# Down phases of a decoder layer: later loads of residual quarters and matrix pieces, and additions spread over steps

## The chip, the cores and the metric

The kernel runs on one core of a Trainium2 chip, in one launch. The metric is device time in microseconds; the median of three runs of the kernel before is 1755.11 us (1754.42 to 1756.94). Five engines with queues of their own share the work: TensorE (PE; its weight load is PEld), VectorE (DVE), ScalarE (ACT), GpSimd (POOL), and SyncE (SP), which issues nearly all DMAs.

## The reference

One layer over x of 1024 tokens by 1024 features, fp32:

```
x = x + 0.5 * swiglu(rmsnorm(x), w_gate1, w_up1, w_down1)      # f = 0
h = rmsnorm(x); P = h @ w_in                                   # the mixer:
x = x + concat(sliding-window attention, gated linear attention, memory attention) @ w_out
x = x + 0.5 * swiglu(rmsnorm(x), w_gate2, w_up2, w_down2)      # f = 1
swiglu(x, g, u, d) = (silu(x @ g) * (x @ u)) @ d,   inner width 2816
```

The change is in the last product of each swiglu, `... @ w_down`, with its `x + 0.5 *`: here called the down phase. There are two, f = 0 (449.6 to 669.2 us of the span) and f = 1 (1532.6 to 1748.8 us).

## The kernel before

**Precision.** Every product is made of three matmuls: each operand is split into a high part (fp32r) and the rest, and high x high, high x low and low x high are summed in PSUM (lines 56 to 58). ACT writes the high part (line 857, `down_op_hi`), DVE subtracts it from the source to get the low part (line 861, `down_op_lo`).

**A down phase** multiplies w_down (2816 x 1024) by the activations (2816 x 1024 tokens) as a 2 x 2 block product with seven products in place of eight (Strassen's scheme in Winograd's form), in the order P1, P2, P6, P5, P7, P4, P3. Each product is 11 steps; step q, from 0 to 76, takes one 128 x 512 tile of w_down (or of a sum of its quarters) as weights in four pieces of 128 columns, and one moving tile of 128 x 512 activations: 4 x 3 = 12 matmuls, each group of three called a tile here. P1, P6, P7 and P4 accumulate in PSUM banks 4 to 7 (`DOWN_X`), P2, P5 and P3 in banks 0 to 3 (`DOWN_Y`). P1, P2 and P5 start their banks anew; the others go on with what is there.

**Operands.** Step q uses operand k = 2q (weights) and k = 2q + 1 (moving tile), in a ring of ten slots, so operands are made five steps ahead. The moving tiles lie in DRAM (`act_dram`) and come back one by one: `load_b(k)` on SP waits until the step that used the slot is done (`down_free`), then issues 256 KB. w_down lies in SBUF in quarters "11", "12", "21", "22" of 11 tiles, loaded in pieces c = 0, 1, 2 of 4, 4 and 3 tiles (`load_wd`, 1 MB or 0.75 MB). In between DVE forms sums of quarters: S3 at steps 5 to 15 (line 868), S2 and S4 at 17 to 27 (lines 878, 881), S1 at 26 to 36 (line 885).

**Additions.** When a product that completes an output quarter (or a part of it) is through, DVE adds 0.5 times its four banks to four tiles of the residual in `xT` (line 908, `down_add`). The residual is loaded again in quarters of 1 MB (`load_x`, halves of features mh and of tokens h). The product that next uses the banks waits for the additions: P6, P5, P7, P4 and P3 wait for those of P1, P2, P6, P7 and of P5 in this order (line 922 and after, `down_added`). Between P7 (steps 44 to 54) and P4 (steps 55 to 65) there is no other product, and both use banks 4 to 7.

**Order of work.** All is written out by hand: `down_vector` is DVE's order, `down_scalar` ACT's, `down_sync` SP's, `down_tensor` PE's. DVE at iteration q makes operands 2q + 10 and 2q + 11; these need step q to be done. In phase f = 0, ACT also squares and scales finished residual tiles for the mixer (`SQUARE_AT`, `SPLIT_AT`), POOL sums them, and POOL makes `spans_raw` from `masks_f` once that has landed.

Of the kernel before, what the change touches and what calls it, by code (L numbers as in the profile page):

```python
# [23 lines left out]
PAIRS = F // (2 * P)  # L24
# [18 lines left out]
RING, DOWN_RING, LEAD = 7, 10, 5  # L43
# [4 lines left out]
DOWN_STEPS = PAIRS * len(DOWN_PRODUCTS)  # L48
# [12 lines left out]
def build(nc, x_in, mem_in, w_gate1, w_up1, w_down1, w_proj, w_mem, w_out, w_gate2, w_up2, w_down2, gains_in,  # L61
# [3 lines left out]
    with ctx:  # L65
# [26 lines left out]
        def place(at, *tensors):  # L92

            skip = [(f"skip{next(places)}", [P, at // 4], F32)] if at else []
            return phase(*skip, *tensors)[len(skip):]
# [44 lines left out]
        masks_f, spans_raw = place(120 * KB, ("masks_f", [P, LEVELS, P], F32), ("spans_raw", [P, LEVELS, P], F32))  # L140
# [26 lines left out]
        DOWN_X, DOWN_Y = 4, 0  # L167
# [43 lines left out]
        masks_landed, span_built, spans_stored = sem("masks_landed"), sem("span_built"), sem("spans_stored")  # L211
# [16 lines left out]
        def upper(t, l):  # L228

            s = P >> (l + 1)  # L230
            return t.rearrange("p (a u c) -> p a u c", u=2, c=s)[:, :, 1, :]
# [578 lines left out]
        def down_slot(k):  # L810
            return (k + RING) % DOWN_RING
# [28 lines left out]
        def down_source(f, k):  # L840

            (name, _), j, moving = down_item(k)
            if moving or name == "P6":
                return down_raw[:, down_slot(k), 1, :]
            return wd_tile(f, {"P1": "11", "P2": "12", "P5": "21", "P7": "11", "P4": "22", "P3": "12"}[name], j)
# [13 lines left out]
        def down_op_lo(dve, f, k):  # L859
            dve.wait_ge(op_hi, Base(f).down_op + k + 1)  # L860
            nc.vector.tensor_tensor(down_ring[:, down_slot(k), 1, :], down_source(f, k),  # L861
                                    down_ring[:, down_slot(k), 0, :].bitcast(F32), ALU.subtract).then_inc(op_ready, 1)
# [20 lines left out]
        def down_s1(dve, f, j):  # L883
            dve.wait_ge(wd_summed["S3"], Base(f).wd_sum + j + 1)
            nc.vector.tensor_tensor(wd_tile(f, "21", j), wd_tile(f, "21", j), wd_tile(f, "22", j), ALU.add
                                    ).then_inc(wd_summed["S1"], 1)


        EVICTS = {"P1": (0, 0, 0, DOWN_X), "P2": (4, 0, 0, DOWN_Y), "P6": (8, 0, 1, DOWN_X), "P7": (12, 1, 1, DOWN_X),
                  "P4": (20, 1, 0, DOWN_X), "P3": (24, 0, 1, DOWN_Y)}  # L890
        FINAL = {(0, 0): 4, (1, 1): 16, (1, 0): 20, (0, 1): 24}

        def x_final(f, m, h):
            return Base(f).evict + FINAL[m // 4, h] + m % 4 + 1

        def down_add(dve, f, p, n, mh, h, bank, j):
            b = Base(f)
            m = 4 * mh + j
            if j < 3:
                dve.wait_ge(tile_done, b.tile + 3 * p + j + 1)  # L900
            else:
                dve.wait_ge(step_done, b.step + PAIRS * (p + 1))
            if j == 0:
                dve.wait_ge(xr_landed[2 * mh + h], 16 * (f + 1))
            if n in (4, 16, 20, 24):
                dve.wait_ge(down_added, b.evict + {4: 0, 16: 12, 20: 0, 24: 8}[n] + j + (1 if n != 20 else 0))
            dst = part(xT, m, h)
            nc.vector.scalar_tensor_tensor(out=dst, in0=ps[:, bank + j, :], scalar=0.5, in1=dst,
                                           op0=ALU.mult, op1=ALU.add).then_inc(down_added, 1)
# [38 lines left out]
        def down_vector(dve, f):  # L948
            b = Base(f)
            for k in range(NEARLY, DOWN_RING):  # L950
                down_op_lo(dve, f, k)
            for q in range(DOWN_STEPS):
                if f == 0 and q == 40:
                    dve.wait_ge(masks_landed, 16)
                    for l in range(SPLITS):
                        nc.vector.tensor_copy(masks[:, l, :].rearrange("p (a c) -> p a c", c=P >> (l + 1)),
                                              upper(masks_f[:, l, :], l)).then_inc(masks_ready, 1)
                name = DOWN_PRODUCTS[q // PAIRS][0]
                if q % PAIRS == PAIRS - 1 and name != "P5":
                    n, mh, h, bank = EVICTS[name]  # L960
                    for j in range(4):
                        down_add(dve, f, q // PAIRS, n, mh, h, bank, j)
                    if name == "P7":
                        for j in range(4):
                            down_add(dve, f, q // PAIRS - 1, 16, 1, 1, DOWN_Y, j)
                if 0 <= q - 17 < PAIRS:
                    down_s24(dve, f, q - 17)
                for k in (2 * q + DOWN_RING, 2 * q + DOWN_RING + 1):
                    if k < 2 * DOWN_STEPS:
                        down_op_lo(dve, f, k)  # L970
                if 0 <= q - 5 < PAIRS:
                    down_s3(dve, f, q - 5)
                if 0 <= q - 26 < PAIRS:
                    down_s1(dve, f, q - 26)
                if f == 0:
                    for c in LOW_AT.get(q, ()):
                        norm_vector(dve, 1, *norm_steps(1)[c])

        def load_wd(sp, f, q, c):

            rows = ffn_weights[f][2].rearrange("(j p) m -> p j m", p=P)
            j0 = PAIRS if q[1] == "2" else 0
            half = slice(0, HALF) if q[0] == "1" else slice(HALF, D)
            for j in range(4 * c, min(4 * c + 4, PAIRS)):
                sp.dma_start(wd_tile(f, q, j), rows[:, j0 + j, half]).then_inc(wd_landed[q][c], 16)  # L985

        def load_b(sp, f, k):
            (_, r), j, _ = down_item(k)
            down_free(sp, f, k)
            sp.wait_ge(act_stored[r], 16 * (Base(f).pair + j + 1))  # L990
            sp.dma_start(down_raw[:, down_slot(k), 1, :], act_rows(r, j)
                         ).then_inc(b_landed[down_slot(k) // 2], 16)

        def load_x(sp, f, mh, h):
            src = (x_in, x_dram)[f].rearrange("(m p) t -> p m t", p=P)
            sp.dma_start(xT[:, 4 * mh:4 * mh + 4, h * HALF:(h + 1) * HALF],
                         src[:, 4 * mh:4 * mh + 4, h * HALF:(h + 1) * HALF]).then_inc(xr_landed[2 * mh + h], 16)

        def down_sync(sp, f):
            b = Base(f)  # L1000
            sp.wait_ge(prod_done, b.prod + OPS * (PAIRS - 1) + 4)
            for c in range(3):
                load_wd(sp, f, "11", c)
            load_b(sp, f, 1)
            sp.wait_ge(prod_done, b.prod + OPS * (PAIRS - 1) + 6)
            load_wd(sp, f, "21", 0)
            for k in (3, 5, 7):
                load_b(sp, f, k)
            load_wd(sp, f, "12", 0)
            for r in ("B22", "B21"):  # L1010
                store_act(sp, f, r, PAIRS - 1)
            load_b(sp, f, 9)
            load_wd(sp, f, "12", 1)
            for r in ("T1", "T2", "T3", "T4"):
                store_act(sp, f, r, PAIRS - 1)
            load_b(sp, f, 11)
            load_wd(sp, f, "12", 2)
            load_b(sp, f, 13)
            load_wd(sp, f, "21", 1)
            load_b(sp, f, 15)  # L1020
            for r in ("B11", "B22", "B21", "T1", "T2", "T3", "T4"):
                sp.wait_ge(act_stored[r], 16 * (b.pair + PAIRS))
            load_x(sp, f, 0, 0)
            load_b(sp, f, 17)
            load_wd(sp, f, "21", 2)
            for c in range(3):
                load_b(sp, f, 19 + 2 * c)
                load_wd(sp, f, "22", c)
            for c, (mh, h) in enumerate(((0, 1), (1, 1), (1, 0))):
                load_b(sp, f, 25 + 2 * c)  # L1030
                load_x(sp, f, mh, h)
            load_b(sp, f, 31)
            if f == 0:
                sp.dma_start(masks_f[:], masks_in).then_inc(masks_landed, 16)
            for k in range(33, 2 * DOWN_STEPS, 2):
                load_b(sp, f, k)
                if f == 0 and k in (91, 97, 103):
                    sp.wait_ge(masks_ready, SPLITS)
                    sp.wait_ge(bias_stored, 16)
                    unit_sync(sp, (k - 91) // 6)  # L1040
# [64 lines left out]
        def part(tensor, m, h):  # L1105
            return tensor[:, m, h * HALF:(h + 1) * HALF]
# [1286 lines left out]
```

## Time and profile before

| what | value |
| --- | --- |
| median of 3 runs | 1755.11 us |
| the profiled execution | 1753.94 us, its span 1752.1 us |
| PE / PEld / DVE / ACT / POOL busy | 97% / 79% / 65% / 41% / 30% |
| mean granted clock of PE | 0.993 |
| DMA over the span | 191.69 MB, 109 GB/s |
| moving tiles from act_dram | 154 issues of 256 KB |

Times of the trace are from the start of the span; 1.84 us of the profiled execution lie outside it. A matmul's duration in the trace (0.39 us) overlaps its neighbours; what counts is the distance of starts. A PE start that is late behind its neighbour is a loss, and the bracket behind a row names the releaser. "DMA share" is the busy share of the core's 16 DMA engines.

### The profile page before, as it was taken

Reading aid. Unit: us, or ns where it says so; the run is one execution under the profiler, and the core shown is the slowest. Engines: PE = TensorE matmul, PEld = TensorE weight load, DVE = VectorE, ACT = ScalarE, POOL = GpSimd, SP = SyncE. Lnnn points to the kernel's source line nnn. Section 1 sums busy time; section 2 is a strip of 40 time slices with the busy share of each in tenths; the row PEclk is TensorE's granted clock in tenths of the full one; section 3 lists DMA queues with packets and bytes.
Section 4 is the critical chain, followed back from the end, with each engine's and each line's share of the span. In section 5 each row is a group of like instructions: output and inputs, shape, how many; then the busy total and the mean of one; then the engine's idle time right before and its main releaser. Section 6 shows DMA issues by size and latency. Waiting matters only on the chain.

```text
span 1752.1 us, 24811 instructions
## 1 busy us (share of the span) xinstructions
PE 1708.0 (97%) x8295; PEld 1385.7 (79%) x8295; DVE 1131.4 (65%) x1582; ACT 718.6 (41%) x1350; POOL 532.4 (30%) x432
## 2 busy tenths in 40 slices
PE   7999999999999999999989999999999999999999
PEld 4888888888778789887756678888888888878877
DVE  8975556545499686247868872986565555559654
ACT  5533333333344463142257842443333333334442
POOL 0454455444130141000036612045554444310000
PEclk9999999999999999999989999999999999999999
DMA  7142222334853331120100032223223322593334
GB/s 200 59 162 91 102 90 98 116 122 144 312 196 99 121 98 66 49 84 24 37 1 2 14 121 90 79 84 104 90 102 118 116 102 90 173 378 95 98 91 162
DMA packets 101693, 191.69 MB, mean 109 GB/s; under 512 B 11491, under 2 KB 13972, under 8 KB 101612
## 3 DMA queue, kind: packets, MB, share of 16 engines
q1 hardware_dynamic: 100528, 188.48, 31.4%
q0 software_dynamic: 848, 2.10, 0.9%
q8 instruction: 47, 0.77, 0.2%
q14 instruction: 34, 0.28, 0.0%
q10 hardware_dynamic: 236, 0.06, 0.0%
HBM read 139.74 MB, written 50.86 MB: 109 GB/s over the span
## 4 chain that ended last, share of the span: by engine, by line
PE 91%; DMA 3%; DVE 2%; ACT 2%; POOL 1%; issue 1%; SPq 1%; ACTq 0%; DVEq 0%
PE ps L56 28%; PE ps L58 28%; PE ps L57 28%; DMA down_raw<-act_dram 3%; PE ps L1595 1%; PE ps L1566 1%; PE ps L1286 1%; ACT glu L1730 1%; POOL Pg L1933 1%; PE ps L1547 1%; PE ps L2298 1%; PE ps L1644 0%; PE ps L1632 0%; PE ps L1365 0%; SPq L985 0%
## 5 line engine op out<-in xcount | busy, mean ns | idle before, releaser
L488 DVE TENSOR_TENSOR ring<-w_raw,ring 128x512 fp32r<-128x512 f32 x240 | 238.0, 1006 | 219.4 <-ACT ring L483 219.2
L58 PE MATMUL ps<-hiT,ring 128*128 128x512 f32 x672 | 261.4, 389 | 0.0
L56 PE MATMUL ps<-hiT,ring 128*128 128x512 f32 x672 | 261.4, 389 | 0.0
L56 PE MATMUL ps<-down_ring 128*128 128x512 f32 x616 | 242.5, 394 | 10.0 <-DVE down_ring L861 5.8
L57 PE MATMUL ps<-loT,ring 128*128 128x512 f32 x640 | 249.0, 389 | 0.0
L57 PE MATMUL ps<-down_ring 128*128 128x512 f32 x616 | 240.5, 390 | 0.0
L58 PE MATMUL ps<-down_ring 128*128 128x512 f32 x616 | 240.3, 390 | 0.0
L56 PE MATMUL ps<-hiB,ring 128*128 128x512 f32 x576 | 224.9, 390 | 0.0
L58 PE MATMUL ps<-hiB,ring 128*128 128x512 f32 x576 | 224.1, 389 | 0.0
L483 ACT ACTIVATE ring<-w_raw 128x512 fp32r<-128x512 f32 x240 | 150.5, 628 | 175.8 <-PE ps L58 163.4
L861 DVE TENSOR_TENSOR down_ring<-down_raw,down_ring 128x512 fp32r<-128x512 f32 x176 | 126.9, 732 | 124.9 <-ACT down_ring L857 124.7
L857 ACT ACTIVATE down_ring<-down_raw 128x512 fp32r<-128x512 f32 x176 | 108.6, 629 | 233.2 <-DMA down_raw<-act_dram 183.7
L504 POOL TENSOR_TENSOR w_raw<-w_raw 128x512 f32<-128x512 f32 x40 | 58.3, 1461 | 313.4 <-DVE ring L488 295.2
L57 PE MATMUL ps<-loB,ring 128*128 128x512 f32 x384 | 149.4, 389 | 0.0
L56 PEld LDWEIGHTS ps<-down_ring 128*128 128x128 f32 x616 | 115.9, 188 | 41.2 <-DVE down_ring L861 17.5
L56 PEld LDWEIGHTS ps<-hiT,ring 128*128 128x128 f32 x672 | 126.1, 188 | 26.3 <-issue 0.2
L58 PEld LDWEIGHTS ps<-hiT,ring 128*128 128x128 f32 x672 | 126.1, 188 | 26.1
L57 PEld LDWEIGHTS ps<-loT,ring 128*128 128x128 f32 x640 | 120.1, 188 | 25.1
L58 PEld LDWEIGHTS ps<-down_ring 128*128 128x128 f32 x616 | 116.0, 188 | 24.3
L57 PEld LDWEIGHTS ps<-down_ring 128*128 128x128 f32 x616 | 116.1, 188 | 23.7
L56 PE MATMUL ps<-hT_hi,p_hi 128*128 128x512 f32 x320 | 132.3, 413 | 2.5 <-DVE p_lo L1216 2.5
L56 PEld LDWEIGHTS ps<-hiB,ring 128*128 128x128 f32 x576 | 108.1, 188 | 22.8 <-issue 0.5
(257 smaller groups left out, 3015.9 us busy)
## 6 DMA issues: line engine op xcount, KB each, us to landing
down_raw<-act_dram SPq DMA_DIRECT2D x154, 256.0 KB, 2.6
w_raw<-in_w_gate SPq DMA_DIRECT2D x88, 256.0 KB, 3.0
w_raw<-in_w_up SPq DMA_DIRECT2D x88, 256.0 KB, 3.2
act_dram<-actT SPq DMA_DIRECT2D x88, 256.0 KB, 2.0
act_dram<-act SPq DMA_DIRECT2D x66, 256.0 KB, 2.0
wd<-in_w_down SPq DMA_DIRECT2D x44, 256.0 KB, 5.5
wd_mirrored<-in_w_down SPq DMA_DIRECT2D x33, 256.0 KB, 5.8
p_raw<-in_w_proj SPq DMA_DIRECT2D x15, 512.0 KB, 3.6
```

Source lines behind the costliest of these rows:

```text
L56: nc.tensor.matmul(out, w_hi, x_hi, start=first, stop=False, skip_group_check=resumed)
L57: nc.tensor.matmul(out, w_hi, x_lo, start=False, stop=False, skip_group_check=resumed)
L58: return nc.tensor.matmul(out, w_lo, x_hi, start=False, stop=last, skip_group_check=resumed)
L483: nc.scalar.activation(ring[:, e % RING, 0, :], op_source(e), ACT.Copy).then_inc(op_hi, 1)
L488: nc.vector.tensor_tensor(ring[:, e % RING, 1, :], op_source(e), ring[:, e % RING, 0, :].bitcast(F32), ALU.subtract).then_inc(op_ready, 1)
L504: nc.gpsimd.tensor_tensor(w_of(x, "11"), w_of(x, "11"), w_of(x, "21"), ALU.subtract).then_inc(w_summed, 1)
L857: nc.scalar.activation(down_ring[:, down_slot(k), 0, :], down_source(f, k), ACT.Copy).then_inc(op_hi, 1)
L861: nc.vector.tensor_tensor(down_ring[:, down_slot(k), 1, :], down_source(f, k), down_ring[:, down_slot(k), 0, :].bitcast(F32), ALU.subtract ...
L1286: nc.tensor.matmul(head_bank(i, w), head_ones[:, :], head_buffer(i, w), start=True, stop=True).then_inc(head_summed, 1)
L1547: mm = nc.tensor.matmul(ps[:, SCORE_BANK[u] + g, at], qT[r, 2 * u + jj, blk(n)], kT[r, keys], start=True, stop=True)
L1566: mm = nc.tensor.matmul(ps[:, SPAN_BANK + c, :], log_a[:, n, :], spans[:, 4 * c:4 * c + 4, :], start=True, stop=True)
L1595: tr = nc.tensor.transpose(ps[:, TURN_BANK[u] + kt, i * P:(i + 1) * P], P_of[u][:, i, kt * P:(kt + 1) * P], ident[:, :])
```

## The change

Two edits, for both phases.

SP's order: before, all pieces of w_down and all four residual quarters were issued behind the first moving tiles, up to k = 29. Now they are issued behind fixed moving tiles: the pieces by `WD_BEHIND` (k = 17 to 43), the residual quarters by `X_BEHIND` (k = 21, 55, 79, 113). As load_b(k) waits for step (k - 11) / 2 to be done, each piece now has a place in time too. The masks (f = 0) come behind k = 35 instead of 31.

DVE's order: before, the four additions of a product stood together, ahead of the operands of the product's last iteration, and those of P5 behind those of P7. Now those of P1, P2, P6 and P5 stand one by one behind the operands of four iterations, those of P7 between the two operands of iteration 53, those of P4 and P3 as before.

```
-                if q % PAIRS == PAIRS - 1 and name != "P5":
+                if name in ("P4", "P3") and q % PAIRS == PAIRS - 1:
                     n, mh, h, bank = EVICTS[name]
                     for j in range(4):
                         down_add(dve, f, q // PAIRS, n, mh, h, bank, j)
-                    if name == "P7":
-                        for j in range(4):
-                            down_add(dve, f, q // PAIRS - 1, 16, 1, 1, DOWN_Y, j)
...
                     if k < 2 * DOWN_STEPS:
                         down_op_lo(dve, f, k)
+                    if k == 2 * (AT_ONCE * PAIRS + PAIRS - 2) + DOWN_RING:
+                        n, mh, h, bank = EVICTS["P7"]
+                        for j in range(4):
+                            down_add(dve, f, AT_ONCE, n, mh, h, bank, j)
+                p, j = (q + 1) // PAIRS - 1, (q + 1) % PAIRS
+                if p in LATER and j < 4:
+                    n, mh, h, bank = LATER[p]
+                    down_add(dve, f, p - (p == AT_ONCE), n, mh, h, bank, j)
...
+        WD_BEHIND = {17: ("21", 2), 19: ("12", 1), 25: ("12", 2), 29: ("22", 0), 37: ("22", 1), 43: ("22", 2)}
+        X_BEHIND = {21: (0, 0), 55: (0, 1), 79: (1, 1), 113: (1, 0)}
...
-            load_wd(sp, f, "12", 1)
...
-            load_wd(sp, f, "12", 2)
...
-            load_x(sp, f, 0, 0)
-            load_b(sp, f, 17)
-            load_wd(sp, f, "21", 2)
-            for c in range(3):
-                load_b(sp, f, 19 + 2 * c)
-                load_wd(sp, f, "22", c)
-            for c, (mh, h) in enumerate(((0, 1), (1, 1), (1, 0))):
-                load_b(sp, f, 25 + 2 * c)
-                load_x(sp, f, mh, h)
...
+            for k in range(17, 2 * DOWN_STEPS, 2):
                 load_b(sp, f, k)
+                if k in WD_BEHIND:
+                    load_wd(sp, f, *WD_BEHIND[k])
+                if k in X_BEHIND:
+                    load_x(sp, f, *X_BEHIND[k])
+                if f == 0 and k == 35:
+                    sp.dma_start(masks_f[:], masks_in).then_inc(masks_landed, 16)
```

SP's queue in phase f = 0, from the moving tile of step 7 (k = 15) on, before. `down_raw` is a moving tile, `wd21` a tile of that quarter, `xT` a residual quarter:

```order
L991 DMA down_raw<-act_dram 128x512 [waits act_storedB11,step_done]
L996 DMA xT<-in_x 128x4x512 [waits act_storedT2,act_storedT1,act_storedT3,act_storedB21,act_storedT4,act_storedB22,act_storedB11]
L991 DMA down_raw<-act_dram 128x512 [waits act_storedB11,step_done]
L985 DMA wd21<-in_w_down1 128x512 x3
L991 DMA down_raw<-act_dram 128x512 [waits act_storedB11,step_done]
L985 DMA wd22<-in_w_down1 128x512 x4
L991 DMA down_raw<-act_dram 128x512 [waits act_storedB11,step_done]
L985 DMA wd22<-in_w_down1 128x512 x4
L991 DMA down_raw<-act_dram 128x512 [waits act_storedB21,step_done]
L985 DMA wd22<-in_w_down1 128x512 x3
L991 DMA down_raw<-act_dram 128x512 [waits act_storedB21,step_done]
L996 DMA xT<-in_x 128x4x512
```

The same queue from the moving tile of step 8 (k = 17) on, after:

```order
L998 DMA down_raw<-act_dram 128x512 [waits act_storedT3,act_storedT2,act_storedT4,act_storedT1,step_done,act_storedB21,act_storedB11,act_storedB22]
L992 DMA wd21<-in_w_down1 128x512 x3
L998 DMA down_raw<-act_dram 128x512 [waits act_storedB11,step_done]
L992 DMA wd12<-in_w_down1 128x512 x4
L998 DMA down_raw<-act_dram 128x512 [waits act_storedB11,step_done]
L1003 DMA xT<-in_x 128x4x512
L998 DMA down_raw<-act_dram 128x512 [waits act_storedB21,step_done] x2
L992 DMA wd12<-in_w_down1 128x512 x3
L998 DMA down_raw<-act_dram 128x512 [waits act_storedB21,step_done] x2
L992 DMA wd22<-in_w_down1 128x512 x4
L998 DMA down_raw<-act_dram 128x512 [waits act_storedB21,step_done] x3
```

Quarter "22" moved from behind the moving tiles of steps 9 to 11 to behind those of steps 14, 18 and 21; the second to fourth residual quarters are not in this stretch any more.

DVE's queue around the end of P7, before (operands of steps 57 and 58, then the additions of P7 and of P5):

```order
L861 TENSOR_TENSOR down_ring<-wd22,down_ring 128x512 [waits op_hi]
L861 TENSOR_TENSOR down_ring<-down_raw,down_ring 128x512 [waits op_hi]
L908 SCALAR_TENSOR_TENSOR xT<-ps,xT 128x512 [waits xr_landed3,tile_done]
L908 SCALAR_TENSOR_TENSOR xT<-ps,xT 128x512 [waits tile_done] x2
L908 SCALAR_TENSOR_TENSOR xT<-ps,xT 128x512 [waits step_done]
L908 SCALAR_TENSOR_TENSOR xT<-ps,xT 128x512 [waits down_added,xr_landed3,tile_done]
L908 SCALAR_TENSOR_TENSOR xT<-ps,xT 128x512 [waits down_added,tile_done] x2
L908 SCALAR_TENSOR_TENSOR xT<-ps,xT 128x512 [waits down_added,step_done]
L861 TENSOR_TENSOR down_ring<-wd22,down_ring 128x512 [waits op_hi]
```

The same place after, from the weights of step 58 (k = 116) on:

```order
L861 TENSOR_TENSOR down_ring<-wd22,down_ring 128x512 [waits op_hi]
L910 SCALAR_TENSOR_TENSOR xT<-ps,xT 128x512 [waits xr_landed3,tile_done]
L910 SCALAR_TENSOR_TENSOR xT<-ps,xT 128x512 [waits tile_done] x2
L910 SCALAR_TENSOR_TENSOR xT<-ps,xT 128x512 [waits step_done]
L861 TENSOR_TENSOR down_ring<-down_raw,down_ring 128x512 [waits op_hi]
L861 TENSOR_TENSOR down_ring<-wd22,down_ring 128x512 [waits op_hi]
L861 TENSOR_TENSOR down_ring<-down_raw,down_ring 128x512 [waits op_hi]
L910 SCALAR_TENSOR_TENSOR xT<-ps,xT 128x512 [waits down_added,xr_landed3,tile_done]
L861 TENSOR_TENSOR down_ring<-wd22,down_ring 128x512 [waits op_hi]
L861 TENSOR_TENSOR down_ring<-down_raw,down_ring 128x512 [waits op_hi]
L910 SCALAR_TENSOR_TENSOR xT<-ps,xT 128x512 [waits down_added,tile_done]
```

P7's additions moved from behind the moving operand of step 58 (k = 117) to ahead of it; P5's moved behind the operands of steps 59 to 62.

## Rows read from the trace of the kernel before

**Rows 1.** The page: the chain that ended last, share of the span by engine.

```profile
PE 91%; DMA 3%; DVE 2%; ACT 2%; POOL 1%; issue 1%; SPq 1%; ACTq 0%; DVEq 0%
```

**Rows 2.** PE's waits, 430 to 680 us: waiting line, releaser, total us, times, longest.

```profile
PE ps L56 <- DVE down_ring L861: 3.9, 5, 1.7
PE ps L56 <- DVE xT L908: 2.0, 1, 2.0
```

**Rows 3.** The same, 1510 to 1752 us.

```profile
PE ps L56 <- DVE down_ring L861: 2.0, 5, 1.2
```

**Rows 4.** Timeline of PE: start us, duration us, engine, line, operation.

```profile
449.60 0.39 PE L56 MATMUL ps<-down_ring 128*128 128x512 f32 x1
...
520.52 0.39 PE L56 MATMUL ps<-down_ring 128*128 128x512 f32 x1
...
523.24 0.39 PE L56 MATMUL ps<-down_ring 128*128 128x512 f32 x1
...
669.18 0.33 PE L56 MATMUL ps<-p_hi,hT_hi 128*128 128x384 f32 x1
...
1532.64 0.39 PE L56 MATMUL ps<-down_ring 128*128 128x512 f32 x1
...
1748.57 0.39 PE L58 MATMUL ps<-down_ring 128*128 128x512 f32 x1
```

**Rows 5.** Timeline of PE where P4 begins, both phases; idle before in brackets.

```profile
607.65 0.47 PE L56 MATMUL ps<-down_ring 128*128 128x512 f32 x1 [1.97 <-DVE xT L908]
...
608.85 0.63 PE L57 MATMUL ps<-down_ring 128*128 128x512 f32 x1
...
1688.84 0.47 PE L56 MATMUL ps<-down_ring 128*128 128x512 f32 x1 [2.00 <-DVE xT L908]
```

**Rows 6.** Windows: busy us of PE, PEld, DVE, ACT, POOL; PEclk, DMA share, GB/s.

```profile
470.00:490.00 20.00, 18.04 (x76) 13.65 (x75) 10.16 (x16) 6.92 (x12) 0.00 (x0) 1.00 1.05 406
...
590.00:620.00 30.00, 28.03 (x118) 22.70 (x116) 20.44 (x27) 16.74 (x28) 7.12 (x5) 0.94 0.31 88
```

**Rows 7.** Line L991, issues of moving tiles, 462 to 486 us: landing.

```profile
DMA to landing us min/median/max: 5.7/10.5/12.0
```

**Rows 8.** The same, 560 to 605 us.

```profile
DMA to landing us min/median/max: 2.5/2.6/3.4
```

**Rows 9.** Line L996, issues of residual quarters: first and last start, landing.

```profile
L996 SPq DMA_DIRECT2D xT<-in_x x4: 378/570/2617, 462.8 to 481.7; - x4
...
DMA to landing us min/median/max: 7.4/11.4/14.0
```

**Rows 10.** Line L985, issues of matrix tiles, 450 to 490 us.

```profile
L985 SPq DMA_DIRECT2D wd<-in_w_down x25: 424/433/1219, 450.2 to 472.8; - x25
```

**Rows 11.** Line L1187, projection loads of 512 KB, 565 to 600 us: landing.

```profile
DMA to landing us min/median/max: 3.5/3.6/3.8
```

**Rows 12.** Timeline of DVE around the end of P7, both phases.

```profile
604.69 0.69 DVE L861 TENSOR_TENSOR down_ring<-wd,down_ring 128x512 fp32r<-128x512 f32 x1 [0.44 <-ACT down_ring L857]
606.21 0.69 DVE L861 TENSOR_TENSOR down_ring<-down_raw,down_ring 128x512 fp32r<-128x512 f32 x1 [0.83 <-ACT down_ring L857]
606.82 4.87 DVE L908 SCALAR_TENSOR_TENSOR xT<-ps,xT 128x512 f32<-128x512 f32 x8
...
1684.88 0.69 DVE L861 TENSOR_TENSOR down_ring<-down_raw,down_ring 128x512 fp32r<-128x512 f32 x1 [1.68 <-ACT down_ring L857]
1685.49 0.68 DVE L861 TENSOR_TENSOR down_ring<-wd_mirrored,down_ring 128x512 fp32r<-128x512 f32 x1
...
1688.01 4.87 DVE L908 SCALAR_TENSOR_TENSOR xT<-ps,xT 128x512 f32<-128x512 f32 x8
```

**Rows 13.** DVE and POOL side by side, 622 us.

```profile
621.92 2.58 POOL L1216 TENSOR_TENSOR p_lo<-p_raw,p_hi 128x1024 fp32r<-128x1024 f32 x1 [0.24 <-ACT p_hi L1206]
...
622.16 2.89 DVE L861 TENSOR_TENSOR down_ring<-wd,down_ring 128x512 fp32r<-128x512 f32 x1
```

**Rows 14.** Line L698, a DVE addition with one input in PSUM.

```profile
L698 DVE TENSOR_TENSOR G<-ps,G x60: 676/683/692, 77.2 to 1531.4; 128x512 f32<-128x512 f32 x60
```

More of the change, by code:

```diff
@@ L890, in build @@
                   "P4": (20, 1, 0, DOWN_X), "P3": (24, 0, 1, DOWN_Y)}
+        AT_ONCE = 4
+        LATER = {0: EVICTS["P1"], 1: EVICTS["P2"], 2: EVICTS["P6"], AT_ONCE: (16, 1, 1, DOWN_Y)}
         FINAL = {(0, 0): 4, (1, 1): 16, (1, 0): 20, (0, 1): 24}
@@ L1022, in down_sync @@
                 sp.wait_ge(act_stored[r], 16 * (b.pair + PAIRS))
-            load_x(sp, f, 0, 0)
-            load_b(sp, f, 17)
-            load_wd(sp, f, "21", 2)
-            for c in range(3):
-                load_b(sp, f, 19 + 2 * c)
-                load_wd(sp, f, "22", c)
-            for c, (mh, h) in enumerate(((0, 1), (1, 1), (1, 0))):
-                load_b(sp, f, 25 + 2 * c)
-                load_x(sp, f, mh, h)
[L1032 to L1035, printed above, removed]
-                load_b(sp, f, k)
+            for k in range(17, 2 * DOWN_STEPS, 2):
+                load_b(sp, f, k)
+                if k in WD_BEHIND:
[4 more added lines that the diff above has]
+                    sp.dma_start(masks_f[:], masks_in).then_inc(masks_landed, 16)
                 if f == 0 and k in (91, 97, 103):
```

## Prediction

> **What bounds the kernel now.** I read the chain that ended last first: 91% of it is PE [rows 1]. So only time in which PE waits, or runs slowly, can be won. The waits of PE in the two down phases come next: in f = 0 it waits for operands made by DVE, 5 times, and once 2.0 us for an addition; in f = 1 again 5 waits for operands [rows 2, 3] and one of 2.00 us for an addition [rows 5]. Such a list counts idle time only, so I measure the whole loss by the starts of matmuls in PE's timeline. In calm running a step takes 523.24 − 520.52 = 2.72 us [rows 4], 12 × 0.2267; 77 steps take 209.5 us. Phase f = 0 runs from 449.60 to 669.18, 219.6 us; f = 1 from 1532.64 to 1748.57 + 0.23, 216.2 us [rows 4]. The losses are 10.1 and 6.7 us, together 16.8 us. That is all that the change can win inside the phases.
>
> **Where the 16.8 us lie.** Two places. First, P4's start: the first matmul of P4 stood 1.97 us in f = 0 and 2.00 us in f = 1 behind DVE's additions [rows 5], with slower starts about 2.2 us each. In f = 0 the matmuls behind it last 0.63 us instead of 0.39, and the window has a granted clock of 0.94 over 30 us [rows 5, 6]: some 3.5 us at the lower of PE's two levels (1.2 instead of 2.4 GHz), half of them lost, 1.7 us. In f = 1 a wait of the same length was followed by no such drop. Together 2.2 + 2.2 + 1.7 = 6.1 us. Second, the rest, 16.8 − 6.1 = 10.7 us, are the waits for operands at steps 6 to 15 of each phase (about 6.2 and 4.5 us).
>
> The reason of the second is the DMA. From 470 to 490 us its share is 1.05 at 406 GB/s, and PE is busy 18.04 of 20 us [rows 6]. Moving tiles issued between 462 and 486 us land after 10.5 us in the median; between 560 and 605 us they land after 2.6 [rows 7, 8]. In the crowded stretch 25 matrix tiles are issued up to 472.8 us and four residual quarters up to 481.7 us, 10.7 MB in 32 us, when moving tiles need only 0.26 MB per step [rows 9, 10]. The reserve can be read at a calm place: the operands of step 57 in f = 1 were complete when DVE had done its row at 1684.88, at 1685.57; P4 (step 55) would begin, without its wait, at 1688.84 − 2.2 = 1686.6, and step 57 two steps later, at 1692.1 [rows 5, 12]: 6.5 us. So a moving tile may land 2.6 + 6.5 = 9.1 us after its issue before PE waits; 10.5 is over that, 3.4 (the longest of the calm stretch) is not.
>
> **The change, part by part.**
>
> *Matrix pieces.* The same transfers, moved. Behind k = 17 to 43 they are released by steps 3 to 16, one piece of 1 MB or less in 1 to 4 steps. Over steps 3 to 16 (14 steps, 38 us) the load is 6 pieces (5.5 MB), 14 moving tiles (3.7 MB), a residual quarter and the masks (1.6 MB): 10.8 MB, 284 GB/s, against the 406 GB/s that the trace reaches. Early it is denser: from step 3 to 7 three pieces and a quarter. Each piece is needed late. Tightest is "12" piece 1: issued after step 4 (near 463 us, 449.6 + 5 × 2.72) and needed at iteration 10 (near 479), 16 us; the slowest quarter of the crowd took 14.0 [rows 9]. I expect landings of 3 to 6 us and no wait: −10.7 us. From both sides: nothing is won if landings stay above 9.1 us; 10.7 us is the most.
>
> *Residual quarters.* The first comes after step 5 (near 466) and is needed at iteration 10 (near 479), 13 us against 14.0 for the slowest in the crowd and 7.4 for the fastest [rows 9]; the others have over 30 us. The fourth (k = 113) is issued after step 51, one step ahead of the moving tile k = 115, which stands in ACT's and DVE's queues before the additions of P7. Projection loads of 0.5 MB land in 3.6 us, 1.0 us later than 0.25 MB [rows 8, 11]; and the longest landing of a moving tile beside them is 3.4, so 0.8 us late. For a quarter of 1 MB with a whole step's head start I take 0.3 us in each phase; ends 0 and 1.5 us (two such delays).
>
> *Additions of P7.* Now they stand behind the weights k = 116 and ahead of the moving tile k = 117, which waits for its DMA. In f = 0 the first began at 606.82; the weights' row ends near 605.30 (604.69 + the 0.61 between starts), 1.52 us earlier; PE's loss goes from 2.2 to 0.7 us. In f = 1 it moves from 1688.01 to 1686.10, 1.91 us; the loss goes to 0.3 us [rows 12]. The tiles they wait for are done by then: the first tile of step 54 ends about 2 us before the step. With an idle time of 0.6 us in place of 1.97 I expect no clock drop, as none followed the waits of up to 1.7 us [rows 2]. Sum: 6.1 − 1.0 = −5.1 us, and + 0.6 for the delay above. Operand 117 comes 2.4 us later than without the additions, out of a reserve of 6.5.
>
> *Additions of P1, P2, P6, P5.* The same 16 instructions, none of them waited for at once: P6, P5, P7 and P3 begin 11 or more steps after the product in question. Spread, they cost DVE 0.60 us per step. Iterations 21 to 24 of f = 0 then hold five operations, 3.1 us per step of 2.72: 1.5 us out of a reserve of 6.5 that before was eaten up by late tiles. 0 us.
>
> *Masks.* Issued after step 12 (near 485 us), as before, but into a calmer DMA; POOL's spans begin up to 7 us sooner. 0 us.
>
> **Sum.** 16.8 lost now; 1.0 remains at P4, 0.6 for the fourth quarter, 0.3 for slow starts here and there: −14.9 us. The profiled execution had 1753.9, so 1739.0; the median of the runs lies 1.2 us above it: **1740.2 us**.
>
> **A rule weighed against the trace.** P5's additions of f = 0 now fall on iterations 54 to 57, where POOL forms the first low parts of the projection. A POOL operation there lasts 2.58 us, and DVE's subtraction beside it 2.89 instead of 0.69 [rows 13]. Blocked like this, two additions would use 2 × 2 = 4 us, and how much of the reserve of 6.5 is left there no row here says: the stall lies between 0 and 4, for a rival I take 2.5. But an addition on DVE with one input in PSUM never took over 0.692 us in 60 executions over the whole kernel [rows 14], POOL busy or not, and `down_add` is of that kind; so I add nothing.
>
> The Trainium skill, page "SBUF — State Buffer", section "Who interferes with whom", says the same in general: a DVE instruction with two SBUF inputs contends with a GpSimd instruction that reads SBUF, one with at most one SBUF input does not. By that rule the term is 0; the trace agrees.
>
> **Rivals.**
>
> *A, the start stays crowded.* Up to step 7 three pieces and a quarter still come together, behind the stores of the last activations. Then part of the waits of steps 6 to 10 stay. For it: the windows are full from 450 us on. Against it: two pieces (1.8 MB, 4.5 us at 406 GB/s) and one quarter left this stretch. Price: about 1.2 us in f = 0 and 1.0 in f = 1, up to 4 in all: 1742.4 to 1744.
>
> *B, P4 waits as long as before.* If ACT's high part for k = 116 comes later than I think (in f = 0 a norm operation stands before it) or the fourth quarter delays k = 115 by 1.5 us, about 2 × 1.5 us and the clock drop's 1.7 return: 1744.9.
>
> *C, DVE becomes the bound in f = 0.* The blocked additions above (2.5 us) or iterations 17 to 27 beside POOL's spans: 1742.7.
>
> *D, slower.* The price of a piece lies in the piece, not in the crowd: a lone 1 MB transfer ahead of a moving tile holds it as long as the crowd does. Then each of 20 pieces (six and four per phase) makes a tile land 10.5 to 11.4 us late where 9.1 is free: 20 × 1.4 to 2.3, 28 to 46 us, in place of 14.9 won; about 1768 to 1786 us. It decides from a landing of 9.1 us, and the change comes out slower from 10 us. Against it: 0.5 MB delayed tiles by 0.8 us at most [rows 8, 11].
>
> *E, nothing is won.* The gain is given back in the mixer between the phases, whose waits are on other engines: near 1754. Against it: nothing there is timed by anything but the end of phase f = 0, and phase f = 1 ends the kernel.
>
> **Chances.** Forecast 0.68, A 0.15, B 0.07, C 0.03, D 0.03, E 0.04. What a measurement can tell from no change is 0.2%, 3.5 us: faster means under 1751.6. Forecast, A, B and C are all faster, 0.93; E is the same, 0.04; D slower, 0.03. Range: the low end is all 16.8 us won, 1738.3, less 1.3 for the spread of the runs; the high end takes in A, B and two of them together: 1737 to 1747.
>
> **What would show it.** In the profile after: landings of moving tiles in the first 15 steps under 6 us; no wait of PE for an operand at steps 6 to 15; one wait at P4 of 0.6 us (f = 0) and about 0.2 us (f = 1), no granted clock under 1 in f = 0's phase; phases of about 210.8 and 210.1 us; DVE with idle time between 470 and 510 us. Wrong would be: landings over 9 us behind a piece (D), additions of P5 over 0.7 us (C), or phases that short with a total that is not (E).

## The result and the profile after

The changed kernel takes 1738.05 us (median of 4 runs, 1736.32 to 1740.66) against 1756.03 us (4 runs); the ratio is 0.9909, interval 0.9893 to 0.9924, so 13 to 19 us less. Forecast were 1740.2 us and a range of 1737 to 1747. The profiled execution was the slowest of the four, 1740.66 us, span 1738.8.

The page, the chain that ended last (answers to [rows 1]):

```profile
PE 94%; DVE 2%; ACT 2%; POOL 1%; DMA 1%; issue 1%; ACTq 0%; DVEq 0%
```

The DMA's part fell from 3% to 1%, PE's rose from 91 to 94%. PE's waits in phase f = 0, and then in f = 1 (answers to [rows 2, 3]; line, releaser, total us, times, longest):

```profile
PE ps L56 <- DVE xT L910: 1.2, 1, 1.2
```

```profile
PE ps L56 <- DVE xT L910: 2.7, 1, 2.7
```

The ten waits for operands are gone. One wait per phase is left, P4 for the additions of P7, shorter in f = 0 and longer in f = 1 than the 2.0 of before. PE's timeline, starts of the phases and of P4 (answers to [rows 4, 5]):

```profile
448.90 0.39 PE L56 MATMUL ps<-down_ring 128*128 128x512 f32 x1
...
599.86 0.47 PE L56 MATMUL ps<-down_ring 128*128 128x512 f32 x1 [1.17 <-DVE xT L910]
...
659.79 0.33 PE L56 MATMUL ps<-p_hi,hT_hi 128*128 128x384 f32 x1
...
1521.46 0.39 PE L56 MATMUL ps<-down_ring 128*128 128x512 f32 x1
...
1673.95 0.47 PE L56 MATMUL ps<-down_ring 128*128 128x512 f32 x1 [2.73 <-DVE xT L910]
...
1675.90 0.63 PE L57 MATMUL ps<-down_ring 128*128 128x512 f32 x1
...
1735.30 0.39 PE L58 MATMUL ps<-down_ring 128*128 128x512 f32 x1
```

Phase f = 0 lasts 210.9 us, f = 1 214.1; less 209.5 for 77 calm steps the losses are 1.4 and 4.6 us, where they were 10.1 and 6.7 before the change. In f = 1 the matmuls behind the wait last 0.63 us in place of 0.39: the lower of PE's two clock levels, which in the kernel before followed the wait of f = 0. The window around it has a mean granted clock (PEclk, the third number from the end) of 0.94:

```profile
1660.00:1690.00 30.00, 27.27 (x114) 22.06 (x113) 16.34 (x26) 10.86 (x19) 0.00 (x0) 0.94 0.36 115
```

Of the 13.3 us between the two profiled executions 10.8 lie in the phases, 1.8 between them (669.2 to 1532.6 before, 659.8 to 1521.5 after), 0.7 ahead of them.

The windows (answer to [rows 6]; PE, PEld, DVE, ACT, POOL, PEclk, DMA share, GB/s), and the landings of moving tiles issued from 460 to 486 us (to [rows 7]):

```profile
470.00:490.00 20.00, 20.00 (x90) 16.54 (x89) 14.92 (x25) 9.28 (x18) 1.31 (x3) 1.00 0.88 315
...
1530.00:1550.00 20.00, 20.00 (x90) 16.55 (x89) 9.37 (x15) 8.55 (x16) 0.00 (x0) 1.00 0.99 360
```

```profile
DMA to landing us min/median/max: 2.7/5.5/9.1
```

PE is busy all 20 us, at a DMA share that is still high. The landings have a median of 5.5 us instead of 10.5. The slowest took 9.1 us, exactly what the prediction worked out as free, and no wait followed.

### The profile page after: what moved, and what is told of

It is laid out like the page before. It is cut to its first block, busy times and chain, and to the rows that moved or that the text cites. A ratio compares the mean times of both kernels' runs of the same rounds, so it can differ in the third digit from the quotient of the medians.

```text
span 1738.8 us, 24811 instructions
## 1 busy us (share of the span) xinstructions
PE 1701.1 (98%) x8295; PEld 1385.8 (80%) x8295; DVE 1128.4 (65%) x1582; ACT 717.3 (41%) x1350; POOL 530.7 (31%) x432
## 4 chain that ended last, share of the span: by engine, by line
PE 94%; DVE 2%; ACT 2%; POOL 1%; DMA 1%; issue 1%; ACTq 0%; DVEq 0%
PE ps L56 29%; PE ps L57 29%; PE ps L58 29%; PE ps L1597 1%; PE ps L1568 1%; PE ps L1549 1%; PE ps L1288 1%; POOL Pg L1935 1%; PE ps L2300 1%; DMA down_raw<-act_dram 1%; ACT glu L1732 0%; PE ps L1646 0%; PE ps L1634 0%; PE ps L1367 0%; DVE p_lo L1218 0%
```

## What held P4 in phase f = 1

The chain of waits before P4 in f = 1 of the changed kernel, from the issue of moving tile k = 115 on (start us, duration us, what):

```profile
1665.81 5.41 DMA down_raw<-act_dram
...
1671.24 0.64 ACT down_ring L857
...
1672.52 0.69 DVE down_ring L861
1673.20 0.61 DVE xT L910
```

k = 115 took 5.41 us to land, 2.8 more than calm. ACT's and DVE's rows for it stand ahead of those for k = 116, and the additions stand behind both. The fourth residual quarter, issued 2.3 us before it at 1663.47, took 7.1 us. In f = 0 the same quarter took 5.0 and the tile 3.3.

## The experiments

Each kernel is compared with the kernel before, run beside it on the same chip; the medians of the kernel before lay between 1754.76 and 1756.03 us. "Loss" is a phase's length in the profile (first to last matmul of the product) less 209.5 us; it comes from one execution of each kernel.

| kernel | us, median | ratio, interval | loss f = 0 | loss f = 1 |
| --- | --- | --- | --- | --- |
| before | 1756.03 | 1 | 10.1 | 6.7 |
| changed, first | 1738.05 | 0.9909 (0.9893 to 0.9924) | 1.4 | 4.6 |
| changed, again | 1738.48 | 0.9905 (0.9884 to 0.9926) | 1.7 | 1.0 |
| e1, SP's order alone | 1741.10 | 0.9924 (0.9907 to 0.9941) | 2.2 | 2.2 |
| e2, DVE's order alone | 1746.94 | 0.9958 (0.9944 to 0.9972) | 5.9 | 4.9 |
| e3, pieces as before | 1743.06 | 0.9941 (0.9922 to 0.9959) | 4.5 | 4.1 |
| e4, quarters as before | 1741.73 | 0.9927 (0.9908 to 0.9946) | 4.5 | 2.9 |
| f2, quarter behind 107 | 1735.37 | 0.9883 (0.9862 to 0.9904) | 0.6 | 0.3 |
| f3, additions behind 114 | 1733.11 | 0.9878 (0.9856 to 0.9899) | 0.1 | 0 |
| f4, both | 1737.20 | 0.9893 (0.9870 to 0.9916) | 0 | 0 |
| g1, additions in bursts | 1737.12 | 0.9897 (0.9872 to 0.9922) | 1.5 | 1.0 |
| g2, quarter behind 115 | 1736.37, one run | | 0.8 | 0.1 |
| g3, f3 again | 1735.11 | 0.9888 (0.9865 to 0.9910) | 0 | 0 |
| g4, f4 again | 1734.11 | 0.9882 (0.9859 to 0.9904) | 0 | 0 |

**e1: SP's new order alone.** Against the changed kernel:

```
+                if q % PAIRS == PAIRS - 1 and name != "P5":
...
+                    if name == "P7":
+                        for j in range(4):
+                            down_add(dve, f, q // PAIRS - 1, 16, 1, 1, DOWN_Y, j)
...
-                    if k == 2 * (AT_ONCE * PAIRS + PAIRS - 2) + DOWN_RING:
...
-                if p in LATER and j < 4:
```

> SP's new order alone; DVE's order as in the kernel before. Theory (the waits of steps 6 to 15 came from crowded DMA alone): all of them go, no wait of PE for an operand in either phase, 10.7 us won; at P4 the additions stand behind k = 117 and k = 115 lands late behind the fourth quarter, so PE loses there about 2.4 us (f = 0) and 3.6 us (f = 1) plus a clock drop of 1.3, some 1.6 us more than in the changed kernel: about 1740 us, ratio 0.991. Rival (the burst of four additions of P1 took part in them: PE's wait of 1.17 us at 1577.75 came right behind such a burst): waits for operands of 1 to 1.5 us stay per phase, about 1742.5 us.

PE waited twice, once in each phase, and both answers are this row:

```profile
PE ps L56 <- DVE xT L910: 2.0, 1, 2.0
```

The theory held for the early steps: none of the ten waits is left, although the bursts of four additions are still there. The rival falls. At P4 the waits are the 2.0 us of before, not the losses of 2.4 and 3.6 us of the expectation, and no clock drop followed: k = 115 landed after 3.3 us in f = 0 and 3.4 in f = 1, and the additions stood behind k = 117, the later of the two anyway. Its interval overlaps that of the changed kernel, and its loss at P4, 4.4 us in both phases together, lies between the 6.0 and 2.7 us of the changed kernel's two profiles: what DVE's order adds to SP's is not told apart by these runs.

**e2: DVE's new order alone.** SP's order is that of the kernel before. Against the changed kernel (cut):

```
-        WD_BEHIND = {17: ("21", 2), 19: ("12", 1), 25: ("12", 2), 29: ("22", 0), 37: ("22", 1), 43: ("22", 2)}
-        X_BEHIND = {21: (0, 0), 55: (0, 1), 79: (1, 1), 113: (1, 0)}
...
+            for c, (mh, h) in enumerate(((0, 1), (1, 1), (1, 0))):
+                load_b(sp, f, 25 + 2 * c)
+                load_x(sp, f, mh, h)
```

> DVE's new order alone; SP's order as in the kernel before, so the fourth quarter is long there when P7 ends. Theory: the waits of steps 6 to 15 stay (about 10.7 us, at most 1.5 us less per phase without the burst); P4 begins 0.6 to 0.7 us late in f = 0 and 0.3 in f = 1, without a clock drop, 5.1 us won: about 1751 us, ratio 0.997. Rival (P4's wait does not depend on the place of the additions but on ACT's high parts): P4 waits 2 us as before, about 1755 us.

PE's waits in f = 0:

```profile
PE ps L56 <- DVE down_ring L861: 2.2, 6, 0.9
PE ps L56 <- DVE xT L910: 0.5, 1, 0.5
```

The waits for operands stay: with their slow starts they cost 4.9 and 4.6 us, 9.5 in all, against 10.1 before (6.0 and 4.1, the sums of late starts in the first 60 us of a phase). P4 waits 0.5 us in f = 0 (0.7 lost) and not at all in f = 1, as forecast for a fourth quarter that is out of the way, and no clock drop followed. Inside the phases 6.0 us are won where 5.1 were expected; the ratio gives 4.9 to 9.8. The rival (P4 waits 2 us as before) falls.

**e3 and e4: one half of SP's change.** Both are shown against the changed kernel, cut. In e3 the pieces of w_down stand where they stood before (and with them the masks of f = 0):

```
-        WD_BEHIND = {17: ("21", 2), 19: ("12", 1), 25: ("12", 2), 29: ("22", 0), 37: ("22", 1), 43: ("22", 2)}
...
+            for c in range(3):
+                load_b(sp, f, 19 + 2 * c)
+                load_wd(sp, f, "22", c)
```

In e4 the quarters do:

```
-        X_BEHIND = {21: (0, 0), 55: (0, 1), 79: (1, 1), 113: (1, 0)}
+        X_BEHIND = {25: (0, 1), 27: (1, 1), 29: (1, 0)}
...
+            load_x(sp, f, 0, 0)
             for k in range(17, 2 * DOWN_STEPS, 2):
```

> The changed kernel, but the pieces of w_down at their places of before; only the residual quarters and DVE's order are as changed. Theory (a sum of traffic: either half relieves the DMA): 6.6 MB of matrix tiles stay in the stretch, some 340 GB/s with moving tiles and stores, landings of 5 to 8 us, at most 2 us of waits left per phase; P4 as late as in the changed kernel: 1738 to 1742 us. Rival (the quarters of 1 MB in one DMA do no harm, the small pieces do): most of the 10.7 us stays, about 1748 us.

> The changed kernel, but the residual quarters at their places of before (three behind k = 25, 27, 29, the first ahead of k = 17); the pieces of w_down and DVE's order are as changed. Theory: 4.2 MB of quarters in the stretch, landings of 5 to 9 us, at most 2 us of waits per phase; no quarter near P7's end, so P4 loses only 0.7 and 0.3 us and no clock drop: 1734 to 1738 us, faster than the changed kernel. Rival (quarters make the crowd): waits of 3 to 5 us per phase stay, about 1743 us.

Landings of moving tiles issued from 462 to 486 us, e3:

```profile
DMA to landing us min/median/max: 2.6/6.9/10.6
```

and e4:

```profile
DMA to landing us min/median/max: 5.8/8.3/10.9
```

Late starts in the early steps add up to 3.0 us in each phase of e3 and to 3.2 and 2.7 in e4 (f = 0, f = 1): 6.0 and 5.9 us, against 10.1 before and 0 with both. Each half wins about 4 us, and together they win 10. Both kinds of loads take part, as the theory said, but I had expected at most 2 us left per phase, and both times lie above what was expected (1743.06 over 1738 to 1742, 1741.73 over 1734 to 1738). The reserve is used up already by the slowest tile (10.6 and 10.9 us, over 9.1), whatever the median. PE's waits in f = 0 of e4 show that it is now a single one:

```profile
PE ps L56 <- DVE down_ring L861: 1.8, 1, 1.8
PE ps L56 <- DVE xT L910: 0.5, 1, 0.5
```

Each rival put the harm in one kind of load alone. Each kind left alone does about the same harm, so neither holds, though the 3.2 us of e4's f = 0 lie within the 3 to 5 of its rival. That the harm goes by the bytes was not tested by itself.

**f1: the changed kernel again; f2: the fourth quarter behind k = 107; g2: behind k = 115.**

```
-        X_BEHIND = {21: (0, 0), 55: (0, 1), 79: (1, 1), 113: (1, 0)}
+        X_BEHIND = {21: (0, 0), 55: (0, 1), 79: (1, 1), 107: (1, 0)}
```

That is f2; g2 has 115 in place of 107, and f1 has no edit.

> The changed kernel again, as the measure for the three beside it. Theory: 1738 us within 2 us; P4 of f = 1 waits 2.5 to 3 us behind the late landing of k = 115 in this profile too. Rival (the 2.73 us of the first profile were a chance of that execution): 0.3 to 1.5 us.

> One number: the fourth residual quarter behind k = 107 instead of 113. Theory (the fourth quarter holds the moving tile k = 115, whose row stands ahead of P7's additions on DVE): k = 115 lands after 2.6 us, P4 loses 0.7 us in f = 0 and 0.3 in f = 1, no clock drop; 4 to 5 us less than the changed kernel in this profile's terms, about 1734 us. Rival (P4's wait has another cause): same time as the changed kernel.

> The fourth quarter behind k = 115, so that k = 117 lands about 0.7 us late and k = 115 in 2.6 us. Theory (only operands ahead of P7's additions on DVE count): P4 loses 0.6 us in f = 0 and 0.3 in f = 1, as with the quarter behind k = 107. Rival (a quarter anywhere near the end of P7 disturbs P4): 1.0 to 1.7 us each as in the changed kernel.

In f1 the quarter landed after 5.2 us in f = 1 and k = 115 after 3.5; P4 waited there

```profile
PE ps L56 <- DVE xT L910: 0.8, 1, 0.8
```

So the 2.73 us of the first profile, with the clock drop behind them, belong to that execution: here my rival was right. Seven of the profiled kernels have the quarter behind k = 113, which makes 14 phases: k = 115 landed after 3.3 to 3.7 us in 13 of them and after 5.4 in this one. What comes each time is the smaller delay. With the quarter behind k = 107, or behind 115, P4 loses 0.6 or 0.8 us in f = 0 and 0.3 or 0.1 in f = 1, where the changed kernel lost 1.4 and 1.7, and 1.0 at best: k = 115 is the tile that counts, as its rows stand ahead of the additions, and a late k = 117 costs nothing (behind 115 it landed after 3.3 and 3.6 us). g2 was run once, and the losses are from one execution of each.

**f3 and f4, and once more g3 and g4: P7's additions one iteration earlier**, in f4 and g4 with the quarter behind 107.

```
-                    if k == 2 * (AT_ONCE * PAIRS + PAIRS - 2) + DOWN_RING:
+                    if k == 2 * (AT_ONCE * PAIRS + PAIRS - 3) + DOWN_RING:
```

> P7's additions one iteration earlier on DVE, behind the weights k = 114 and ahead of the moving tile k = 115; the fourth quarter stays behind k = 113. Theory: the additions now wait for PE's tiles alone; P4 loses at most 0.2 us in both phases whatever k = 115 does; 4.5 to 5.5 us less than the changed kernel, about 1733 us. Operand 115 comes 3 to 5 us later, out of a reserve of 6.5 of which the late landing takes 2.8: if that is too little, step 57 waits 0 to 1.5 us in f = 1 (rival: the wait only moves there).

> Both edits. Theory: no wait of PE at P4 nor after it, phases of 209.5 us; 0 to 0.5 us faster than the better of the two, about 1733 us, the fastest version. Rival: waiting for PE's tiles DVE falls behind for good and waits for operands of 1 us or more appear at steps 57 to 63.

> P7's additions one iteration earlier, again, for the time beside its twin. Theory: both phases lose nothing; executions fall into two groups some 6 us apart (1730 to 1737 us) by how often PE's clock drops in the mixer between the phases, and the median says little between the twins. Rival: it is faster than the twin by 4 us again, as the medians of the first measurement were (1733.1 and 1737.2).

> The twin, with the fourth quarter behind k = 107. Theory: the same time as the other within 2 us, 1730 to 1737 us, no loss in either phase. Rival: 4 us slower again.

DVE in f = 1 of f3:

```profile
1661.09 0.69 DVE L861 TENSOR_TENSOR down_ring<-wd_mirrored,down_ring 128x512 fp32r<-128x512 f32 x1
1663.23 2.73 DVE L910 SCALAR_TENSOR_TENSOR xT<-ps,xT 128x512 f32<-128x512 f32 x4 [1.45 <-PE ps L58]
1665.88 0.68 DVE L861 TENSOR_TENSOR down_ring<-down_raw,down_ring 128x512 fp32r<-128x512 f32 x1
```

Now DVE waits 1.45 us for PE's first tile, and PE for nobody: in the windows from 590 to 620 and from 1660 to 1690 us it is busy 30.00 of 30 us. The operands behind the additions are in time, so the rival (the wait moves to step 57) falls. In four profiles the phases lose 0 to 0.1 us. By the phases this is the best version. By the time it is clear for f3 beside f1, measured together: the slowest of f3's six executions took 1735.22 us, and five of f1's six took 1737.52 or more. The ratios are 0.9878 and 0.9888 for f3, 0.9893 and 0.9882 for f4. f4 was not the fastest, as I had expected; the order of the twins turned round at the second measurement, so they are not told apart. Nor do the executions fall into two groups, as g3's theory has it: several of g3 and g4 took 1734 to 1736 us, between the two.

**g1: the additions of P1, P2 and P6 in bursts again.**

```
-                if name in ("P4", "P3") and q % PAIRS == PAIRS - 1:
+                if name in ("P1", "P2", "P6", "P4", "P3") and q % PAIRS == PAIRS - 1:
...
-        LATER = {0: EVICTS["P1"], 1: EVICTS["P2"], 2: EVICTS["P6"], AT_ONCE: (16, 1, 1, DOWN_Y)}
+        LATER = {AT_ONCE: (16, 1, 1, DOWN_Y)}
```

> The changed kernel, but the additions of P1, P2 and P6 together again, ahead of their iteration's operands; P7's and P5's as changed. Theory (spread or not, nobody waits for them and DVE has reserve without the crowd): no wait of PE in steps 6 to 43, losses of the phases as in the changed kernel's second profile (1.7 and 1.0 us), about 1738.5 us. Rival (the spreading is what keeps operands in time): waits of 0.5 to 1.5 us at steps 15 to 17 and 26 to 28.

No wait came at the places of the rival; both losses and the time (1737.12 beside 1738.48, measured at another time) are those of the changed kernel. Spreading these additions is worth nothing that can be measured once the DMA is relieved; with the crowd there it was worth the 0.6 us of e2 at most.

## Why the prediction was right, point by point

*The bound and its size.* The loss of 16.8 us read from PE's starts was all there was in the phases: f3 and f4 win it whole. The late starts divide it a little otherwise than forecast: 10.1 us in the early steps and 6.6 at P4, in place of 10.7 and 6.1.

*Matrix pieces and quarters, −10.7 us.* Held: 10.1 us of late starts became 0, by SP's order alone (e1). The two halves share it about evenly (e3, e4). Landings came out at 2.7 to 9.1 us with a median of 5.5, where I had said 3 to 6: the start is denser than I thought (DMA share 0.99 in f = 1 from 1530 to 1550). Of the signs this one failed. The price of rival A did not come, but with no margin, and so by luck in part: in f3's f = 0 the slowest tile took 9.3 us, and PE started 0.1 us late.

*The fourth quarter, 0.3 us per phase, ends 0 and 1.5 for both.* This term was mis-sized. k = 115 landed 0.7, 1.0, 2.8 and 0.9 us late in the four phases profiled (3.3, 3.6, 5.4 and 3.5 us, less 2.6). Against the 0.7 and 0.3 us expected at P4 without it, the loss there was 1.4 and 1.7 us in f = 0, 4.6 (with the clock drop) and 1.0 in f = 1. I had taken the delay from a transfer of half the size and granted it a head start of a whole step; the quarter itself lasted 5.0 us at best, twice the 2.3 us of head start. Of the signs the one wait at P4 of 0.6 and 0.2 us failed as well: it was 1.2 and 2.7 us in the first profile, 1.5 and 0.8 in the second. All that was to be left in the phases was 1.9 us; the two profiles have 6.0 and 2.7.

*Rival B* came true in the first profile: the quarter delayed k = 115 by more than the 1.5 us that B asks for, the clock drop followed in f = 1, and the phases lost 4.1 us more than forecast, of the 4.7 that B was priced at. In the second profile it did not. I had given it 0.07; that the time still fell into the range is no sign that this part was right.

*P7's additions.* Held where the quarter was away: e2, f2 and g2 lose 0.6 to 0.8 us there in f = 0 and 0 to 0.3 in f = 1, forecast 0.7 and 0.3. The place behind k = 116 was not the best one: behind k = 114 the term is 0. Of the 5.1 us of this term 1.7 were the clock drop of f = 0, and they are not safely the change's: e1 had the waits of 2.0 us and no drop.

*The spread additions, 0 us, and the rule on the shared port.* Held (g1). P5's additions beside POOL in f = 0 of the changed kernel:

```profile
609.93 5.25 POOL L1218 TENSOR_TENSOR p_lo<-p_raw,p_hi 128x1024 fp32r<-128x1024 f32 x2 [0.40 <-ACT p_hi L1208]
```

```profile
610.00 2.90 DVE L861 TENSOR_TENSOR down_ring<-down_raw,down_ring 128x512 fp32r<-128x512 f32 x1
612.83 0.68 DVE L910 SCALAR_TENSOR_TENSOR xT<-ps,xT 128x512 f32<-128x512 f32 x1
613.43 2.29 DVE L861 TENSOR_TENSOR down_ring<-wd,down_ring 128x512 fp32r<-128x512 f32 x1
```

The addition at 612.83, with one input in PSUM, ran in 0.68 us beside POOL's second operation, between two subtractions of 2.90 and 2.29. Rival C falls. The Trainium skill's rule (page "SBUF — State Buffer", section "Who interferes with whom") is borne out here: a DVE instruction with one SBUF input does not contend with a GpSimd instruction that reads SBUF, one with two does.

*Rival D* (the price lies in the piece) falls. Behind the second to fourth quarters the next tile landed after 3.3 to 5.6 us in the changed kernel's two profiles, 0.7 to 3.0 more than calm, and behind the piece at k = 37 after 4.7 and 5.1 us in f = 0: never 9.1. The 0.8 us that I had taken as the most were too few. *Rival E* falls too: between the phases the profiled pair differs by 1.8 us in the change's favour, so nothing was given back.

*The total.* 14.9 us were forecast; the profiled pair differs by 13.3, the medians by 18.0, the ratio says 13 to 19. The medians are no clean measure of the change, as the mean granted clock differs: most executions of the kernel before have 0.992 or 0.993, those of the changed kernel 0.994 to 0.997. In the measurement of f1, executions with the same clock can be put side by side: at 0.995 the kernel before took 1750.74 us and the changed one 1738.27 and 1738.69, at 0.997 1746.40 and 1734.50. That is 12 to 12.5 us, between the 10.8 and 14.0 us that the two profiles won in the phases, and less than the forecast. So the 18.0 us hold some 5 us or more that go with the clock, and the closeness of 1738.05 to the forecast of 1740.2 is luck in part. Whether the change itself raises the clock is open.

## What to carry to other kernels

When a stretch is held up by late DMAs, sum the bytes issued in it and ask when each transfer is first needed. Placing the bulk loads behind the steady stream, one at a time, took the whole wait away here (e1), and each half of the bulk counted (e3, e4). Work that another engine waits for is best put ahead of whatever in its queue waits for a DMA, even if it then waits itself, as long as its queue has reserve and the waiting engine has none (f3). And the slowest landing decides, not the median: 9.1 us gave no wait, 10.6 did.

## What the runs showed of the hardware

Part of the scatter between runs of one kernel is PE's clock in the mixer between the phases. Take two executions of f4's kernel, both without loss in the phases: the first (1731.38 us) took 857.8 us between the phases, the second (g4's profile, 1737.07 us) 863.8. The windows (columns as in [rows 6]) differ in PEclk; phase f = 0 ended at 659.0 and 658.7 us. The first:

```profile
670.00:730.00 60.00, 57.46 (x296) 51.83 (x295) 19.55 (x19) 8.45 (x10) 0.00 (x0) 0.97 0.11 36
...
860.00:910.00 50.00, 42.97 (x382) 30.39 (x380) 35.62 (x105) 28.11 (x94) 23.28 (x32) 0.97 0.01 1
```

and the second:

```profile
670.00:730.00 60.00, 57.46 (x281) 51.84 (x280) 19.28 (x19) 7.68 (x9) 0.00 (x0) 0.91 0.11 36
...
860.00:910.00 50.00, 43.21 (x334) 30.77 (x334) 34.87 (x91) 23.33 (x78) 17.76 (x29) 0.90 0.00 1
```

PE was busy for the same time, but at a lower mean clock, and did less: 281 matmuls in place of 296, 334 in place of 382. The program is the same, so a difference of 2 or 3 us between two kernels here can be nothing but this, and the losses read inside the phases tell more than the medians. What makes the clock differ is not shown. A wait of PE of 1.97 us was followed by the lower clock in f = 0 of the kernel before, one of 2.00 us in f = 1 was not, and in e1 neither of two of 2.0 us was; the one of 2.73 us in the changed kernel was. The length of a wait alone did not decide it.
